# Layer one's running sums over keys as VectorE scans, and attention weights turned by VectorE and moved as squares instead of by TensorE

## The reference, cut to what matters

```python
def stick_breaking_attention(q, k, v):          # per block of 128 queries
    z = jnp.einsum('bhqd,bhkd->bhqk', qi, k).astype(jnp.float32) * scale
    past = key_pos[None, :] < t_idx[:, None]
    log_beta = jax.nn.log_sigmoid(z)
    log_1m_beta = jnp.where(past, jax.nn.log_sigmoid(-z), 0.0)
    tail = lax.cumsum(log_1m_beta, axis=3, reverse=True) - log_1m_beta
    w = jnp.where(past, jnp.exp(log_beta + tail), 0.0)
    return jnp.einsum('bhqk,bhkd->bhqd', w.astype(v.dtype), v)

def moba_attention(q, k, v, k_mean):            # one block: causal softmax
    s_own = jnp.where(own_pos[None, :] <= t_idx[:, None], s_own, NEG_BIG)
    probs = jax.nn.softmax(scores, axis=-1)
    ...

def stick_breaking_layer(x, w_in, w_out):       # moba_layer is alike, with rotary q and shared k, v
    q, k, v, z = jnp.split(x @ w_in, 4, axis=-1)
    o = stick_breaking_attention(split_heads(q), split_heads(k), split_heads(v))
    return (merge_heads(o) * jax.nn.silu(z)) @ w_out

# each layer:  x = layer_norm(alpha * x + y);  x = x + (p @ w_ple) * sigmoid(x @ w_ple_gate)
```

## Time and profile before

| | us |
|---|---|
| median of 3 runs (lowest, highest) | 1145.32 (1145.03, 1145.46) |
| profiled execution | 1142.92 |
| its span, first to last instruction | 1141.2 |
| TensorE matmul busy | 1136.4 (100%) |
| VectorE busy | 746.6 (65%) |
| ScalarE busy | 591.4 (52%) |
| GpSimd busy | 233.4 (20%) |
| DMA, mean rate | 207 GB/s |

### The profile page before, as it was taken

The page is one execution under the profiler, slowest core; times in us unless marked ns, Lnnn a source line. Parts: engine busy times, 40 slices in busy tenths (PEclk is TensorE's granted clock), DMA queues, the critical chain, the costliest instruction groups (busy, mean ns, idle before and its releaser), DMA issues.

```text
span 1141.2 us, 15511 instructions
## 1 busy us (share of the span) xinstructions
PE 1136.4 (100%) x5264; PEld 948.8 (83%) x5264; DVE 746.6 (65%) x795; ACT 591.4 (52%) x669; POOL 233.4 (20%) x475
## 2 busy tenths in 40 slices
PE   9999999999999999999999999999999999999998
PEld 8888888888888888888888888888888888888887
DVE  7665556556556566688788775457766667656873
ACT  6574566457547453555454554555455444434641
POOL 1402221420250300003537654320000010000000
PEclk9999999999999999999999999999999999999999
DMA  9876765775675687456887877764555575763571
GB/s 321 270 223 197 208 205 170 207 221 167 184 221 178 213 295 215 132 181 227 263 272 224 251 240 223 220 215 151 171 171 176 165 240 172 255 199 117 190 258 53
DMA packets 126587, 235.67 MB, mean 207 GB/s; under 512 B 13856, under 2 KB 16160, under 8 KB 126032
## 3 DMA queue, kind: packets, MB, share of 16 engines
q1 hardware_dynamic: 109888, 209.22, 58.6%
q0 software_dynamic: 16368, 25.37, 6.9%
q10 hardware_dynamic: 288, 0.52, 0.1%
HBM read 216.71 MB, written 4.19 MB: 194 GB/s over the span
## 4 chain that ended last, share of the span: by engine, by line
PE 100%; DVE 0%; issue 0%; POOL 0%; DVEq 0%; POOLq 0%
PE acc L1203 31%; PE acc L1205 31%; PE acc L1204 30%; PE aux L1240 2%; PE aux L1233 1%; PE acc L1182 1%; PE aux L1266 1%; PE aux L1280 1%; PE aux L1413 0%; PE aux L1297 0%; PE aux L1205 0%; PE aux L1204 0%; PE aux L1203 0%; PE aux L1255 0%; PE aux L1402 0%; DVE stage L1038 0%
## 5 line engine op out<-in xcount | busy, mean ns | idle before, releaser
L752 DVE TENSOR_TENSOR w_lo<-raw,w_hi 128x1024 fp32r<-128x1024 f32 x388 | 470.3, 1223 | 329.8 <-ACT w_hi L481 329.3
L481 ACT ACTIVATE w_hi<-raw 128x1024 fp32r<-128x1024 f32 x388 | 409.8, 1060 | 437.8 <-PE acc L1205 360.8
L1203 PE MATMUL acc<-w_hi,act 128*128 128x512 f32 x1532 | 601.4, 393 | 0.1
L1205 PE MATMUL acc<-w_hi,act 128*128 128x512 f32 x1532 | 596.9, 390 | 0.0
L1204 PE MATMUL acc<-w_lo,act 128*128 128x512 f32 x1532 | 596.2, 389 | 0.0
L1205 PEld LDWEIGHTS acc<-w_hi,act 128*128 128x128 f32 x1532 | 287.5, 188 | 61.0
L1203 PEld LDWEIGHTS acc<-w_hi,act 128*128 128x128 f32 x1532 | 287.7, 188 | 58.6 <-issue 0.7
L1204 PEld LDWEIGHTS acc<-w_lo,act 128*128 128x128 f32 x1532 | 287.8, 188 | 58.2
L431 POOL DMA_DIRECT2D heads<-big x192 | 94.1, 498 | 273.8 <-DVE big L773 230.6
L431 POOL DMA_DIRECT2D heads<-v_or_z x64 | 31.4, 498 | 51.9 <-DVE v_or_z L773 39.0
L431 POOL DMA_DIRECT2D stage<-v_or_z x48 | 23.6, 501 | 70.5 <-DVE v_or_z L990 44.0
(11 more groups left out here) (162 smaller groups left out, 671.3 us busy)
## 6 DMA issues: line engine op xcount, KB each, us to landing
raw<-in_w_in_a SPq DMA_DIRECT2D x124, 512.0 KB, 3.9
raw<-in_w_ple_gate SPq DMA_DIRECT2D x64, 512.0 KB, 4.9
raw<-in_w_in_b SPq DMA_DIRECT2D x64, 512.0 KB, 4.8
raw<-in_w_kv SPq DMA_DIRECT2D x64, 512.0 KB, 3.7
raw<-in_w_out_a SPq DMA_DIRECT2D x32, 512.0 KB, 4.6
raw<-in_w_out_b SPq DMA_DIRECT2D x32, 512.0 KB, 4.8
heads<-big POOLq DMA_DIRECT2D x192, 32.0 KB, 3.4
heads<-in_ln_rows POOLq DMA_DIRECT2D x4, 1024.0 KB, 7.7
```

What stands on the lines that cost most here:

```text
L481: nc.scalar.activation(w_hi[:, r], raw[:, r % RAWS], ACT.Copy).then_inc(hi_ready, 1)
L752: nc.vector.tensor_tensor(w_lo[:, r], raw[:, r % RAWS], w_hi[:, r].bitcast(F32), ALU.subtract) \
L1203: nc.tensor.matmul(dst, hi, w_hi[:, r, i], start=begin, stop=False)
L1205: mm = nc.tensor.matmul(dst, lo, w_hi[:, r, i], start=False, stop=end)
```

## The change

Layer one's scores get queries on partitions and keys on columns. The running sum over later keys is then along a row, and VectorE makes it with one backwards scan per half (`tensor_tensor_scan`, multiply by `segments`, then add; `segments` is 1 and is 0 where a new row of keys starts). TensorE's `cumulate` goes, with its triangle and its square of -1, and so do the splitting of the softplus and the multiplication by `past`; the causal mask is added to the scores at once, before the softplus. The finished weights, and layer two's probabilities, now have keys on columns and must be turned: VectorE turns squares of 32 and a new `exchange` with 48 KB DMAs moves them, in both layers; TensorE's `probs_turn` goes. The value products run later and both halves together: behind q3 instead of q0 and q1, behind k6 instead of k3 and k4, and behind pieces 3 and 7 of the output projections for the last groups. In layer two's last v-k pair the gate steps move with them. The last turn of x2 and its splitting move from piece 2 to piece 3 of layer two's first chunk.

```diff
-            def exchange(turned, count, dst, src, moved):
+            def exchange(turned, count, dst, src, moved, width=HT // NS):
...
                     for g in range(NS):
-                        pool.dma_start(dst[g * SQUARE:(g + 1) * SQUARE, a * HT // NS:(a + 1) * HT // NS],
-                                       src[a * SQUARE:(a + 1) * SQUARE, g * HT // NS:(g + 1) * HT // NS]) \
+                        pool.dma_start(dst[g * SQUARE:(g + 1) * SQUARE, a * width:(a + 1) * width],
+                                       src[a * SQUARE:(a + 1) * SQUARE, g * width:(g + 1) * width]) \
                             .then_inc(moved, 16)
...
+                exchange(w_turned, g + 1, w_moved_to, w_turned_to, w_moved, PW)
...
-                pool.wait_ge(scores_ready, g * 2 + 2 * G)
+            for g in range(G):
+                if g > 0:
+                    exchange(p_turned, g, probs_moved, probs_turned, p_moved, PW)
+                    pool.wait_ge(p_moved, g * MOVED)
...
+            exchange(p_turned, G, probs_moved, probs_turned, p_moved, PW)
...
             def stick_weights_hi(k, b):
...
-                act.wait_ge(cum_ready, k * 2 + 2)
-                nc.scalar.activation(w_parts[:, 0, b], prob[:, b, :, 0:T], ACT.Copy).then_inc(weights_hi, 1)
+
+                act.wait_ge(w_moved, k * MOVED + MOVED)
+                nc.scalar.activation(early_keys(w_parts, 0, b), weights_moved_x[:, 4 * b:4 * b + 4], ACT.Copy) \
+                    .then_inc(weights_hi, 1)
...
             def exp_abs(k, b):
-                act.wait_ge(scores_ready, k * 2 + (b + 1))
+                act.wait_ge(masked, k * 2 + (b + 1))
...
             def stick_weights(k, b):
-                act.wait_ge(masked, k * 2 + (b + 1))
-                nc.scalar.activation(prob[:, b], scores_of(b), ACT.Exp).then_inc(w_ready, 1)
+                act.wait_ge(stick_log, k * 2 + (b + 1))
+                nc.scalar.activation(prob[:, b], prob[:, b], ACT.Exp).then_inc(w_ready, 1)
...
             def after_z(k):
-                return {0: [lambda: softplus_hi(k, 0)], 1: [lambda: softplus_hi(k, 1)],
-                        5: [lambda: stick_weights(k, 0)],
-                        6: [lambda: stick_weights(k, 1), lambda: stick_weights_hi(k, 0)],
-                        7: [lambda: stick_weights_hi(k, 1)]}
+                return {1: [lambda: stick_weights(k, 0)], 2: [lambda: stick_weights(k, 1)]}
             def gate_group(k):
-                return {5: [lambda: silu_z_group(k)], 6: [lambda: gated_hi(k, k)]}
+                return {1: [lambda: stick_weights_hi(k, 0), lambda: stick_weights_hi(k, 1)],
+                        5: [lambda: silu_z_group(k)], 6: [lambda: gated_hi(k, k)]}
...
+            def sum_later_keys(k, b):
+
+                backwards = prob[:, b].rearrange("p h c -> p (h c)")[:, ::-1]
                 dve.wait_ge(sp_raw, k * 2 + (b + 1))
-                for h in range(2):
...
+                nc.vector.tensor_tensor_scan(backwards, segments[:, :], backwards, 0.0, ALU.mult, ALU.add) \
+                    .then_inc(sp_summed, 1)
+                dve.wait_ge(sp_summed, k * 2 + (b + 1))
+                nc.vector.tensor_tensor(prob[:, b], scores_of(b), prob[:, b], ALU.subtract).then_inc(stick_log, 1)
...
             def mask_stick(k, b):
-                dve.wait_ge(cum_ready, k * 2 + (b + 1))
+                dve.wait_ge(scores_ready, k * 2 + (b + 1))
                 mask_scores(k, b, not_past)
+
+            def turn_weights(b, ready, count, dst_x, turned):
+
+                dve.wait_ge(ready, count)
+                nc.vector.transpose(dst_x[:, 4 * b:4 * b + 4].rearrange("p (h q) a c -> p h q a c", q=2),
+                                    probs_rows(b, 0, T))
+                last = nc.vector.transpose(dst_x[:, 8 + 2 * b:10 + 2 * b], probs_rows(b, T, SC)[:, :, 0])
+                if b == 1:
+                    last.then_inc(turned, 1)
...
             def v_steps(k, n):
-                return {7: [lambda: values_lo(k), lambda: evacuate_v(n, 0, vn_a), lambda: softplus(k, 0)]}
+                return {6: [lambda: mask_stick(k, 0)],
+                        7: [lambda: mask_stick(k, 1), lambda: values_lo(k), lambda: evacuate_v(n, 0, vn_a),
+                            lambda: softplus(k, 0)]}
...
             def z_steps(k, n):
-                return {0: [lambda: softplus(k, 1)], 1: [lambda: softplus_lo(k, 0)], 2: [lambda: softplus_lo(k, 1)],
-                        4: [lambda: mask_stick(k, 0)], 5: [lambda: mask_stick(k, 1)],
-                        6: [lambda: stick_weights_lo(k, 0)],
-                        7: [lambda: turn_squares(n + PC, 1, zn), lambda: stick_weights_lo(k, 1)]}
+                def turn(b):
+                    turn_weights(b, w_ready, k * 2 + (b + 1), weights_turned_x, w_turned)
+
+                return {0: [lambda: softplus(k, 1), lambda: sum_later_keys(k, 0)], 1: [lambda: sum_later_keys(k, 1)],
+                        2: [lambda: turn(0)], 3: [lambda: turn(1)],
+                        7: [lambda: turn_squares(n + PC, 1, zn)]}
             def gate_steps(k):
-                return {5: [lambda: gate_group(k, k, sz_a)], 6: [lambda: gated_lo(k, k, k + S_OUT[0])]}
...
-            dve.wait_ge(consts_done, 12)
+                return {1: [lambda: stick_weights_lo(k, 0), lambda: stick_weights_lo(k, 1)],
+                        5: [lambda: gate_group(k, k, sz_a)], 6: [lambda: gated_lo(k, k, k + S_OUT[0])]}
...
             dve.wait_ge(tables_landed, 32)
-            pieces(N_Q, N_Q, {2: [last_x2_lo, lambda: find_shift(1), lambda: normalise_x2(0)],
+            pieces(N_Q, N_Q, {2: [lambda: find_shift(1)], 3: [last_x2_lo, lambda: normalise_x2(0)],
...
+            def turn_probs(k, b):
+
+                turn_weights(b, probs_ready, (k - G) * 2 + (b + 1), probs_turned_x, p_turned)
...
             def after_v_b(k, n):
                 return {2: [lambda: keys_lo_b(k)],
-                        4: [lambda: row_max(k, 0)], 5: [lambda: row_max(k, 1), lambda: divide(k, 0)],
-                        6: [lambda: divide(k, 1)],
+                        4: [lambda: row_max(k, 0)], 5: [lambda: divide(k, 0), lambda: turn_probs(k, 0)],
                         7: [lambda: values_lo_b(k), lambda: evacuate_v(n, 1, v_or_z)]}
-            def after_k_b(k):
-                return {0: [lambda: probs_lo(k, 0)], 1: [lambda: probs_lo(k, 1)],
-                        4: [lambda: gate_group(k, k - G, quarter(sz_all, k - G)),
-                            lambda: gated_lo(k, k - G, (k - G) + S_OUT[1])]}
+            def before_v_b(k):
+                return {5: [lambda: row_max(k, 1)], 6: [lambda: divide(k, 1), lambda: turn_probs(k, 1)]}
+
+            def before_k_b(k):
+                return {5: [lambda: probs_lo(k, 0), lambda: probs_lo(k, 1)]}
+
+            def gate_b(k):
+                return {7: [lambda: gate_group(k, k - G, quarter(sz_all, k - G))]}
...
-                    three_passes(s[:, 0:T], lambda i, h=h: k_parts[:, i, h], lambda i, h=h: q_parts[:, i, h], True)
-                    mm = nc.tensor.matmul(s[:, T:SC], k_own[:, h], q_scaled[:, h, P:T], start=False, stop=True,
-                                          skip_group_check=True)
+                    nc.tensor.matmul(s[:, 0:P], q_scaled[:, h, 0:P], kT_x[:, TT * h], start=True, stop=True,
+                                     skip_group_check=True)
+                    mm = three_passes(s[:, P:SC], lambda i, h=h: q_parts[:, i, h], lambda i, h=h: k_parts[:, i, h], False)
...
-            def cumulate(k, b):
-
-                pe.wait_ge(sp_lo, k * 2 + (b + 1))
-                for i, h in enumerate((2 * b, 2 * b + 1)):
-                    s, (hi, lo) = aux_b[:, h], (sp_parts[:, part, b, i] for part in range(2))
-                    for dst, lhs, rhs in ((s[:, 0:SC], neg_upper, hi), (s[:, 0:SC], neg_upper, lo),
-                                          (s[:, P:T], neg_ones, hi[:, T:SC]), (s[:, P:T], neg_ones, lo[:, T:SC])):
-                        mm = nc.tensor.matmul(dst, lhs[:, :], rhs, start=False, stop=True,
-                                              skip_group_check=True)
-                mm.then_inc(cum_ready, 1)
...
             def weigh_step(k, v_chunk):
-                return {0: [lambda: weigh_values(k, 0, v_chunk, v_parts, vn_a, w_parts)],
-                        1: [lambda: weigh_values(k, 1, v_chunk, v_parts, vn_a, w_parts)]}
+                return {3: [lambda: weigh_values(k, 0, v_chunk, v_parts, vn_a, w_parts, weights_moved_x),
+                            lambda: weigh_values(k, 1, v_chunk, v_parts, vn_a, w_parts, weights_moved_x)]}
...
-            def probs_turn(k, b):
-
-                pe.wait_ge(probs_ready, (k - G) * 2 + (b + 1))
-                for i in range(2):
-                    for s in range(3):
-                        mm = nc.tensor.transpose(aux_b[:, 2 * b + i, s * P:(s + 1) * P],
-                                                 prob[:, b, i, s * P:(s + 1) * P], ident[:, :])
```

(37 more changed lines are left out.)

126 lines of the change are left out of this document (58 added, 68 removed).

## The result

The changed kernel took 1153.05 us (median of 7 runs, 1146.29 to 1156.79), the kernel before 1143.78 beside it: a ratio of 1.0074, 95% interval 1.0050 to 1.0099. The forecast was 1131.0 with a range to 1138. It is slower, not faster.

What follows compares the result with a forecast made beforehand. TensorE was taken to bound the kernel, with hardly a gap. The profiled 1142.92 us less 16.3 of work plus 2.0 of waits gave 1128.6, with 2.4 up to the median 1131.0; range 1128 to 1138.

Steps and rivals of the forecast that it cites:

- What leaves TensorE: Running sums 9.5 us, layer two's transposes 5.4, value products together 1.1, layer one's scores 0.3: 16.3 us saved.
- The reads in runs of 32 columns: TensorE's moving reads of keys and turned weights: taken at nothing, upper end +12 us; rival's range 1138 to 1143, chance 0.09.
- Steps 1 to 3: Layer one's chain from scores through splits, softplus and two scans (1.82 us each) to the turn, all turned at 188.2.
- Step 4: Layer one's weight exchange: landing 3.4 us after the last issue, 4.8 at worst; weights ready at 200.3, at worst 201.7.
- The recorded list of what would show the forecast wrong: Signs: longer small blocks, scans over 2 us, 48 KB landings over 5 us, TensorE waiting for weight pieces or piece 12.
- Step 5: TensorE asks behind q3 at 200.05, about when data are ready; wait 0.25 us per group, 0.5 taken, 2.0 in all.
- late exchange in every group: Rival: layer one's exchange lands late, 1.7 to 2.3 us per group, 1136 to 1138 us; chance 0.20 for 1133 to 1138.
- The threshold I worked out for "slower": Rival of a slow scan in layer one: slower from 4.65 us of wait per group, scans of 4.0 us; chance 0.04.
- Layer two: Layer two's turn and exchange were to add nothing: landed at 805.5, second half ready at 809.8, before TensorE asks.
- the 2 us to spare behind k6: Layer two's value products: second half ready at 809.8, TensorE asks behind k6 at 812.0.
- the last projection's piece 12: The gate behind pieces 8 and 9 feeds this piece: ready within 0.1 us of it; a wait over 0.5 would show wrong.
- the forecast's 1129.0 without a wait: Median of the kernel before less the 16.3 us leaving TensorE, with no wait for layer one's exchange.

Runs made afterwards that it cites:

- weigh_5: Changed kernel with layer one's value products behind q5 instead of q3; 1131.75 us, ratio 0.990 to the kernel before.
- light: Changed kernel with layer one's later q and k weight loads and the output projection's first 16 bringing a quarter of their columns, the rest stale; 1128.63 us.
- filled: Changed kernel with 14 further products of 512 columns on TensorE between q3 and its wait for the weights; 1146.29 us.
- narrow: Changed kernel with layer one's weights exchanged in 32 KB DMAs instead of 48 KB, other weights read in place of the rest; 1149.64 us.
- weigh_4: Changed kernel with layer one's value products behind q4 instead of q3; 1135.17 us.

## Why the prediction was wrong

- **What leaves TensorE: right.** In weigh_5 each group of layer one gives back 2.38 us of running sums (9.5 in all), layer two's transposes 1.37 per group (5.5; 5.4 predicted), scores 0.3. Two halves of value products together gave 0.09 us per group instead of 0.14. PE is busy for 1121.4 us there ("near 1120" was forecast); the changed kernel's 1132.1 has the slow stretches in it. The reads in runs of 32 columns cost nothing that shows: a half's scores take 1.15 instead of 1.08 us but the pieces behind are as much quicker, and the value products of four heads take 2.23.
- **Steps 1 to 3, up to the turn: right to 0.1 us**, the scan too. The Trainium skill (DVE: opcode table, instruction layouts, handler registers and perf-mode slots; section Datapath and trigger behaviour) has the built-in scan at half throughput. The trace agrees: 1.75 us for 768 columns, where an ordinary pass takes 0.95.
- **Step 4, the landing: this is the step that failed.** I took 3.4 us after the last issue for 48 KB, and 4.8 at worst, from the 32 KB exchanges of the kernel before. It was 6.3 to 7.0 (6.75, 6.34, 7.00 and 6.91 in the four groups). The words were there ("weight loads catch up at that time and can only add") and were priced at 0.25 us per group, 0.5 in place of 0.25. I had read the kernel before where VectorE had been busy for a long stretch, at 230 GB/s; here VectorE splits several weight pieces back to back once the scans are through (192.17 to 195.6 in group 1), each split frees a buffer, and the loads come as a burst just as the exchange is issued: the DMA share goes from 0.35 over 176 to 192 us to 0.96 over 192 to 204. light puts the loads to the test: a quarter of those bytes, and the landing is 2.1 us. That they come bunched because of VectorE's splits is read from the timeline and not shown; no run changed the order of the splits. The recorded list of what would show the forecast wrong had this sign: landings of the 48 KB exchanges over 5 us.
- **Step 5 was right** (TensorE asks at 204.0; 204.1 predicted), and so the whole 3 us of the landing became a wait, with nothing in hand. The rival "late exchange in every group" had the mechanism but a price of 1.7 to 2.3 us per group. The measured price is 4.1 us of wait per group (4.25 from the end of q3) and more for the clock.
- **The clock was not in the forecast at all.** The kernel before is at 1.00 throughout, and so nothing in its trace gave a price for a stop. The threshold I worked out for "slower" (4.65 us of lateness per group) counted the wait alone; filled shows that about 7 us came on top, without which the changed kernel would be only 0.2% above the kernel before (1.0023, 1.0011 to 1.0034). Even that is not faster, and the threshold itself was too high: the kernel before takes 1143.7 us in these runs and light, without the waits, 1128.6, so waits of 15 us, 3.8 per group, already use up the gain, and 4.3 per group make it slower by the 2.3 us that the threshold asks for.
- **Layer two: right.** Its landing was late as well (ScalarE waits 4.3 us for it, 4 times), but the 2 us to spare behind k6 covered it, and the last projection's piece 12 began 0.04 us late.

The sum with the measured terms, on the changed kernel's own span of 1155.0: 24.6 us of longer blocks and 2.3 of slow pieces behind them leave 1128.1. light, where neither occurs, has a span of 1127.7. That its median of 1128.6 is so near the forecast's 1129.0 without a wait is in part luck. The forecast starts from a median of 1145.32, and the kernel before took 1143.7 beside light; and light's span is 13.5 us under that of the kernel before, though 16.0 us of work left TensorE (9.5, 5.5, 0.3 and 0.7 of value products). The other 2.5 us are small losses that the forecast did not have, among them 0.3 before the first scores (68.33 instead of 67.99) and waits of 0.5 and 0.6 us.

## What to carry to other kernels

When a block moves from the engine that bounds to a chain of others, the chain's last link, here a transfer, must be priced in the traffic that it will meet, and the consumer set behind the worst landing of it: in weigh_5 a place two pieces later in TensorE's order cost nothing and was worth 21 us. A stop of the busiest engine is not priced by its length alone when the granted clock falls behind it; a trace that has no stop cannot give that price. And work out what the landing would have to be for the sign to turn, before trusting a median taken from a quieter stretch.

## What the hardware showed that was not expected

- At waits of 3.6 to 5.2 us in which TensorE did nothing, its granted clock was 0.50 for 3.4 or 6.8 us (changed kernel), and it fell to 0.50 at one of 2.5 us too (narrow); behind waits of 0.9 to 1.8 us (weigh_4) and of 2.1 us (filled) it stayed at 1.00 in the traces. The runs of the changed kernel vary with it: the one of 1146.29 us has a mean clock of 0.999, the one of 1156.79 has 0.990.
- The DMAs of the same 768 KB exchange take 2.1 us to land, in the median of the four groups, in light, and 5.9 in the changed kernel, where the DMA share over group 1's exchange is 0.49 and 0.96; taking a third of the exchange's own bytes away brought it to 5.1 only.
- GpSimd issues the ninth and the fourteenth of layer one's exchanges some 2.3 us after their data are ready, the others after 0.3 us, or up to 1.7 where the exchange before them is still being issued; the cause is open.
